# Strict alternation of channel groups and head pairs in the input projection of a retention and convolution backbone

## The reference

```
p = modulate(x, sh1, sc1) @ w_in[l]              # columns q, k, v, g (512 each), a, b (512 each)
q = apply_rope(split_heads(p[q]), cos, sin)      # 8 heads of 64
k = apply_rope(split_heads(p[k]), cos, sin) * 64 ** -0.5
o_f = retention_scan(q, k, v, lg_f, s_f)         # chunks of 128 tokens, both directions
o_b = retention_scan(flip(q), flip(k), flip(v), lg_b, s_b)
ret  = silu(g) * group_norm(o_f + flip(o_b))
u    = a * sigmoid(b)
conv = silu(layer_norm(depthwise_conv(u, 31 taps) + conv_b))
mix  = concat(ret, conv) @ w_out[l]
x    = layer_norm(alpha * x + g1 * mix); then a squared-ReLU MLP and a second layer norm
```

## Time and profile before

| | |
|---|---|
| median of 3 runs | 3204.29 us (3204.11 to 3205.83) |
| the profiled execution | 3203.33 us, span of its instructions 3201.5 us |
| mean granted TensorE clock | 0.949 |
| PE busy | 2880.6 us, 90% of the span |
| DVE busy | 2234.4 us, 70% |
| ACT busy | 705.1 us, 22% |
| POOL busy | 1026.0 us, 32% |

### The profile page before, as it was taken

The page is one execution under the profiler, slowest core; times in us unless marked ns, Lnnn a source line. Parts: engine busy times, 40 slices in busy tenths (PEclk is TensorE's granted clock), DMA queues, the critical chain, the costliest instruction groups (busy, mean ns, idle before and its releaser), DMA issues.

```text
span 3201.5 us, 36747 instructions
## 1 busy us (share of the span) xinstructions
PE 2880.6 (90%) x12824; PEld 2256.2 (70%) x12824; DVE 2234.4 (70%) x3490; ACT 705.1 (22%) x1400; POOL 1026.0 (32%) x939
## 2 busy tenths in 40 slices
PE   7798999779799999999998499998797999999994
PEld 1387778347588888888886387784476787777873
DVE  0497675376877786868778787742767777877787
ACT  0322323332411111111111333332323111111111
POOL 0133435165421111111113454452553221212124
PEclk9899999889899999999999699998798999999997
DMA  9311112353011111111112211123421111111111
GB/s 362 74 40 48 47 36 100 134 151 93 20 47 40 39 39 39 33 34 38 39 39 27 91 51 52 57 94 135 138 75 47 46 52 39 52 39 52 41 45 66
DMA packets 255715, 215.54 MB, mean 67 GB/s; under 512 B 60736, under 2 KB 203648, under 8 KB 255616
## 3 DMA queue, kind: packets, MB, share of 16 engines
q10 hardware_dynamic: 143112, 125.89, 12.9%
q1 hardware_dynamic: 112504, 88.41, 9.1%
HBM read 191.62 MB, written 22.64 MB: 67 GB/s over the span
## 4 chain that ended last, share of the span: by engine, by line
PE 73%; DVE 12%; issue 6%; POOL 4%; ACT 2%; DMA 2%; SPq 0%; ACTq 0%; POOLq 0%; DVEq 0%
PE bank L515 12%; PE bank L517 11%; PE bank L516 11%; PE bank L953 8%; PE bank L955 8%; PE bank L954 8%; PE bank L591 5%; PE bank L825 2%; DVE work L1584 2%; PE bank L826 2%; PE bank L827 2%; PE bank L884 1%; PE bank L883 1%; DVE x_hl L1355 1%; PE bank L867 1%
## 5 line engine op out<-in xcount | busy, mean ns | idle before, releaser
L1320 POOL TENSOR_TENSOR w_lo<-raw,w_hi 128x1024 fp32r<-128x1024 f32 x120 | 303.4, 2529 | 1175.5 <-ACT w_hi L1176 1175.5
L1586 DVE TENSOR_TENSOR work<-work 128x512 f32<-128x512 f32 x576 | 551.8, 958 | 20.0
L515 PE MATMUL bank<-w_hi,h_hi 128*128 128x512 f32 x1152 | 459.3, 399 | 42.9 <-DVE work L1584 42.9
L953 PE MATMUL bank<-x_hl,w_hi 128*128 128x512 f32 (+1 forms) x1280 | 475.1, 371 | 0.8 <-ACT work L1167 0.5
L954 PE MATMUL bank<-x_hl,w_hi 128*128 128x512 f32 (+1 forms) x1280 | 472.7, 369 | 0.0
L955 PE MATMUL bank<-x_hl,w_lo 128*128 128x512 f32 (+1 forms) x1280 | 472.5, 369 | 0.0
L516 PE MATMUL bank<-w_lo,h_hi 128*128 128x512 f32 x1152 | 452.3, 393 | 0.0
L517 PE MATMUL bank<-w_hi,h_lo 128*128 128x512 f32 x1152 | 452.1, 392 | 0.0
L1584 DVE TENSOR_TENSOR work<-bank,work 128x512 f32<-128x512 f32 x576 | 393.4, 683 | 0.0
L1485 DVE SCALAR_TENSOR_TENSOR bank<-work,bank 128x512 f32<-128x512 f32 (+1 forms) x580 | 366.6, 699 | 3.9
L1563 DVE TENSOR_TENSOR work<-work 128x512 f32<-128x512 f32 (+1 forms) x160 | 125.2, 782 | 349.6 <-ACT work L1167 349.6
(11 more groups left out here) (131 smaller groups left out, 4421.5 us busy)
## 6 DMA issues: line engine op xcount, KB each, us to landing
raw<-in_w_ff ACTq DMA_DIRECT2D x128, 512.0 KB
plain_words<-in_w_ada SPq DMA_DIRECT2D x12, 2048.0 KB
plain_words<-in_w_ada ACTq DMA_DIRECT2D x12, 2048.0 KB
raw<-in_w_in ACTq DMA_DIRECT2D x64, 256.0 KB
raw<-in_w_in ACTq DMA_DIRECT2D x16, 512.0 KB
raw<-in_w_out ACTq DMA_DIRECT2D x16, 512.0 KB
gate_rows<-work SPq DMA_DIRECT2D x72, 64.0 KB, 1.6
retention_rows<-work SPq DMA_DIRECT2D x72, 64.0 KB, 1.5
```

What stands on the lines that cost most here:

```text
L515: nc.tensor.matmul(out_ps, hi, whi, start=first, stop=False)
L953: nc.tensor.matmul(o, slot(mlp_slot(f), 0)[:, wc], x_hi[:, k, cols], start=k == 0, stop=False)
L1320: nc.gpsimd.tensor_tensor(slot(mlp_slot(sl), 1), raw[:, un % 2, :], slot(mlp_slot(sl), 0).bitcast(F32), ALU.subtract).then_inc(w_ready, 1)
L1586: nc.vector.tensor_tensor(X[:, t, hc], X[:, t, hc], y_t[:, yi % 2, :], ALU.add).then_inc(S["y_add"], 1)
```

## The change

The list of groups is put in another order. Nothing else is edited; the planner makes other lists for both layers out of it, and the weight units are numbered in the new order (`UNIT_OF`).

```diff
-GROUPS = [("AB", 0), ("AB", 1), ("Q", 0), ("AB", 2), ("Q", 1), ("AB", 3), ("Q", 2), ("Q", 3)]
+GROUPS = [("AB", 0), ("Q", 0), ("AB", 1), ("Q", 1), ("AB", 2), ("Q", 2), ("AB", 3), ("Q", 3)]
```

## The result

The changed kernel takes 3253.16 us (median of 4 runs, 3252.37 to 3258.14) against 3205.06 (3204.11 to 3206.34) for the kernel before in the same session: ratio 1.0158, 95% interval 1.0145 to 1.0171. It is slower by 48 us; the forecast was 3253 (3232 to 3267). The profiled execution took 3252.42 us with a span of 3250.6, 49.1 us more span than before.

The account below looks back on a forecast made before the run. TensorE, 73% of the chain that ended last, was taken as the bound, stopping at hand-overs, between pairs 2 and 3, and in tails. Layer 0 +30.4 and layer 1 +18.3 gave +48.7 us: 3253 us, range 3232 to 3267.

Parts of the forecast that it names:

- Hand-overs, layer 0: Layer 0, where a channel group follows a pair: three hand-overs at 16.6 us each replace 30.1 us of stops, +19.7 us.
- +5.0 of products: Layer 0: three value, two score and two state products leave the tail for the stream before it, +5.0 us.
- the two VectorE waits stay under 2: Sign of being wrong: layer 0 hand-over waits behind VectorE's taps, forecast at 2.8 and 2.4 us, stay under 2 us.
- Clock rival: Each added wait brings another 3.4 us stretch at half speed, some 10 of them, +12 us, 3265 us; chance 0.14.
- Mask wait, layer 1: Start of layer 1's pair 0: first state product waits 11.4 us for decay masks; with clock, +12.9 us.
- Layer 1 hand-overs: Layer 1, where a channel group follows a pair: three at 7.5 us each instead of 19.4 us, +3.1 us.
- whatever VectorE does: Claim that ScalarE's weight load ahead of the state copies makes every hand-over wait, in layer 1 too, regardless of VectorE.
- Tail of layer 0: After layer 0's last projection: first score 5.3 us earlier, taps delay the fourth by 10.5, clock 0.5; +5.7 us.
- Tail of layer 1: After layer 1's last projection: the last group's 0.5 MB store shares transfer engines with 4 MB of weights, +1.3 us.
- The taps hide: Rival: narrow taps fit VectorE's holes, so 10.1 us of hand-overs and 10.5 of tail fall away, 3232 us; chance 0.17.
- Faster: Rival: pair 2's catch-up leaves layer 0's tail, and with added costs hidden the time is at best 3191 us; chance 0.03.
- No effect: Rival: the sum of TensorE's unchanged work bounds the stage and waits merely move, 3204 us; chance 0.04.

Follow-up runs that it names:

- t: Changed kernel with up to 7 wide taps behind each step of pair 3 in layer 0, leaving none in the tail; 3240.6 us.
- mask run: Changed kernel with layer 1's wide mask exponential and its VectorE product behind step 8 instead of step 3; 3246.8 us.
- h: Changed kernel with up to 7 wide taps behind each step of pairs 0 to 2 in layer 0, none left in hand-overs; 3234.8 us.
- o1: Kernel before with only pair 0 moved early, the last channel group left where it was; 3234.5 us.
- o2: Kernel before with only the last channel group moved between the last two pairs; 3214.2 us.
- loads run: Changed kernel with each step's weight load at the end of that step's actions, except in the last step; 3225.1 us.
- bias-row run: Changed kernel with the four bias rows issued ahead of the last two 2 MB adaLN weight transfers; 3238.1 us.
- all remedies: Changed kernel with no taps in hand-overs or tail, loads behind, bias rows first, and layer 1's masks spread later; 3174.3 us.

## Why the prediction was right, step by step

*Hand-overs, layer 0 (+19.7 with +5.0 of products; measured +24.9).* Per hand-over 16.6 forecast; after, 10.5 of wait and 0.12 x 57.5 = 6.9 of clock, 17.4. The split was wrong: I had 12.1 and 4.5. The second VectorE wait was forecast at 2.4 and is 0.73, because the steps before it run at half speed (255.49 to 258.26, matmuls of 0.63 where they are 0.39 behind) and use up the time. Over the whole stream the waiting grew by 10.1 us (21.3 to 31.3), where the forecast had 15.3, and PE's busy time by 14.8, where it had 4.4 of clock and 5.0 of products. VectorE's round is what I had worked out, 262.80 - 253.41 = 9.39 against 9.4, so the sum held whichever way TensorE spent it. The tail-tap and mask runs say the same: the first VectorE wait of their three hand-overs is 4.04, 3.41 and 4.91 us in t and 2.88, 3.11 and 4.90 in the mask run, and their streams are 418.5 and 417.9 us, as after's. I had given "the two VectorE waits stay under 2" as a sign of being wrong; it was a poor sign, the round is the quantity to watch. That the taps are needed for these two waits is shown by h; the 2.1 us by which the scan is longer beside GpSimd's split lie in the same queue, and stand in both kernels.

*Clock rival (0.14).* The Trainium skill (TensorE: Matmul & The Clock Gate, What's actually happening) has it that throttled is the default and activity lifts it. The trace agrees in part: each layer 0 hand-over is at 0.88 instead of 0.91, but layer 1 repeats its 0.91, 0.96, 0.91 with the same waits, so not every wait is followed by half speed. In layer 0 the rival's half speed did come, some 5 us more than my term for it by the figures above. But it took the place of waiting, since VectorE's round set the length, and did not add to the time. The rival's price was also mis-summed: ten times 1.7 is 17, not 12.

*Mask wait, layer 1 (+12.9).* Forecast 11.4 and 2.0 of clock. Measured 12.59 of wait; and PEclk is 0.52 in the four microseconds behind it. The stream's +18.0 against +17.0 is this. Its place is shown by o1 and o2, its cause in the larger part by the run with the masks later.

*Layer 1 hand-overs (+3.1).* Waits of 0.6 to 0.8, 1.8 and 1.8 to 2.2 each, as forecast; the load as the cause of one of the two near 1.8 is shown by the loads run, where it goes. The other stays, then ended by VectorE, so "whatever VectorE does" was too strong: the load and VectorE's mask product end it at nearly the same time. The size I took, 7.5 for each, was 7.8, 6.1 and 7.7.

*Tail of layer 0 (+5.7; measured +9.1).* This term was mis-sized. Its first marks came as said: adaLN product 14.9 after the last projection (14.5), first score 23.2 (23.1). The fourth score came at 51.7 instead of 47.9. What I left out is a second queue: PE waits 4.40 at 633.39 for the state copy. ScalarE and VectorE of after there:

```profile
631.63 0.39 ACTq L578 DMA_DIRECT2D plain_words<-in_w_ada  x1
632.67 0.63 ACT L1120 ACTIVATE work<-work 64x128 f32<-64x128 f32 x2 [18.95 <-issue]
```

```profile
622.86 7.83 DVE L1485 SCALAR_TENSOR_TENSOR bank<-work,bank 128x256 f32<-128x256 f32 x15
...
630.93 0.67 DVE L1342 TENSOR_TENSOR plain_words<-bank,plain_words 2x512 f32<-2x512 f32 x1
```

The 15 taps delay the adaLN row on VectorE (630.93), the next adaLN load waits for that row on ScalarE (631.63), and the copy of the state, ready long before, stands behind the load (632.67). Delay in one engine's order went through a load into a third engine's. The same 4.27 is in o2, and it is absent in t.

*Tail of layer 1 (+1.3; measured +1.4).* The size is right, but of the reason only part: the bias-row run shows the adaLN weights themselves as the main wait there, on which the 0.5 MB store can weigh as well. The delay goes with the place of the last channel group: its first adaLN product starts 14.5 us after the last projection in o1 and 16.4 in o2 (14.7 before, 16.3 after). That the store is the cause was not tried.

*The rest of the program,* counted as 0, came out 4.3 us shorter. Cut at the same marks, that rest lies between 2333 and 2339 us over all twelve traces, with no order in it that goes with the edits, so the 4.3 can't be told from scatter between executions. The layer 0 tail was 3.4 us too low and the layer 1 stream 1.0, and these cancel against it: the hit to within a microsecond is partly luck, the terms are good to 1 to 4 us.

*Rivals.* "The taps hide" (0.17) fell: without them the hand-overs give 18.3 and the tail 12.5. "Faster" (0.03) was wrong for the change as made, but its first sentence was sound: once waits are removed, this order and o2 do lead, by 9 to 10 us. "No effect" fell with the mask wait.

Open: the 4.18 us (6.15 with all remedies) that stay at pair 0 in layer 1; the first adaLN product of layer 1, which another choice of buffers might release; and the query copy behind a load that waits for its DMA (3.75). The same goes for the scan step that takes 2.40 us beside a split. None was tried further.

## What to carry to other kernels

Before an order is changed, write out for every engine what stands in its queue at each new junction, and follow one level further: a wait on a load or an issue holds back everything behind it on that engine, however ready it is. Compare the rounds of two engines (here 9.4 us of VectorE against 6.9 of TensorE), since the sum is set by the longer round and not by the single waits that the trace shows. And where an order that ought to pay costs time, mend the collisions first, on both orders, and compare them again: here the order that was 48 us slower came out 9 us faster.

## What the runs showed of the hardware that I had not expected

- Four issues of small bias rows took 5.02 us of ScalarE's queue behind two 2 MB issues, 4.10 of it the first one, and 1.23 us ahead of them. The issuing engine itself was held up, and its copies with it.
- Five to seven microseconds lost to the taps in a hand-over show as only 3.5 us of waiting; most of the rest is matmuls at 0.63 instead of 0.39 us behind the waits (granted clock 0.88 over 57 us). Counting brackets alone undersizes such a stall by some two fifths.
- Behind the 12.59 us wait the granted clock was 0.52 (1.2 GHz) for the next microseconds, while in the tail with all remedies, 7 us of scattered waits in 52.5, it stayed at 1.00.
- One step of an 18-step VectorE scan took 2.40 us in place of 0.27 in each of the six hand-overs of after; it began within 0.2 us of the start of GpSimd's 2.4 us split and ended 0.08 us behind it. In the two tails, without a split, the whole scan took 3.61 us.
